# A transformer kernel's first stage: scale vectors spread by TensorE, transfers and splits reordered, first queries turned later

## What is computed

```python
def rms_norm(x, g):
    xf = x.astype(jnp.float32)
    y = xf * lax.rsqrt(jnp.mean(xf * xf, axis=-1, keepdims=True) + NORM_EPS)
    return (y * g.astype(jnp.float32)).astype(x.dtype)
...
mem_n = rmsnorm(mem, norm_mem[layer])
km, vm = jnp.split(mem_n @ w_kv, 2, axis=-1)
...
h = rms_norm(x, attn_norm_g[l])
proj = jnp.einsum('bsd,de->bse', h, w_in[l])
qa, ka, va, qb, kb, vb, f_logit, g_logit = jnp.split(proj, bounds, axis=-1)
qa = partial_rope(rms_norm(split_heads(qa, N_MOBA_HEADS), moba_q_norm_g[l]), pos)
```

## Time and profile before

| | us |
|---|---|
| median of 3 executions | 869.7 |
| lowest and highest | 868.4, 872.04 |
| the profiled execution | 871.05 |
| its span, first to last instruction | 868.8 |
| PE busy | 797.1 (92%) |
| DVE busy | 550.6 (63%) |
| ACT busy | 485.9 (56%) |
| POOL busy | 86.6 (10%) |

### The profile page before, as it was taken

How to read it: one execution, slowest core, us unless ns; L and a number is a source line. 1 busy time by engine, 2 the same in 40 slices (tenths; PEclk the granted TensorE clock), 3 DMA queues, 4 the chain that set the end, 5 groups by cost and what they waited for, 6 DMA issues and landing times.

```text
span 868.8 us, 10702 instructions
## 1 busy us (share of the span) xinstructions
PE 797.1 (92%) x3811; PEld 647.7 (75%) x3811; DVE 550.6 (63%) x817; ACT 485.9 (56%) x743; POOL 86.6 (10%) x50
## 2 busy tenths in 40 slices
PE   4989999999799999999999798796859999999998
PEld 3777788777588888888887577663637888888886
DVE  5676676567556777776463477687673666665650
ACT  4755656666236777774264744342543677776630
POOL 0023000000000000000000056644231000000000
PEclk9989999999999999999999899798969999999999
DMA  8766333344237655456383533221001675554550
GB/s 303 292 203 198 103 116 119 97 147 140 68 120 251 211 193 193 151 170 204 105 270 124 179 98 97 78 68 49 25 25 48 215 237 182 177 184 173 191 165 24
DMA packets 70566, 130.21 MB, mean 150 GB/s; under 512 B 5534, under 2 KB 17142, under 8 KB 70142
## 3 DMA queue, kind: packets, MB, share of 16 engines
q1 hardware_dynamic: 69662, 124.90, 44.2%
q10 hardware_dynamic: 864, 4.78, 1.5%
HBM read 128.61 MB, written 1.05 MB: 149 GB/s over the span
## 4 chain that ended last, share of the span: by engine, by line
PE 74%; DVE 11%; ACT 7%; DMA 4%; issue 2%; POOL 1%; SPq 1%; ACTq 0%; DVEq 0%; POOLq 0%
PE acc L478 20%; PE acc L480 20%; PE acc L479 20%; DMA b_raw<-in_w_in 2%; DVE b_wlo L1186 2%; PE banks L579 2%; PE banks L704 2%; PE banks L539 2%; PE banks L564 2%; PE banks L717 1%; DMA b_raw<-in_w_mem_kv 1%; ACT b_whi L825 1%; PE banks L552 1%; PE banks L543 1%; PE banks L566 1%
## 5 line engine op out<-in xcount | busy, mean ns | idle before, releaser
L1186 DVE TENSOR_TENSOR b_wlo<-b_raw,b_whi 128x1024 fp32r<-128x1024 f32 (+4 forms) x222 | 253.1, 1179 | 102.8 <-ACT b_whi L825 101.4
L825 ACT ACTIVATE b_whi<-b_raw 128x1024 fp32r<-128x1024 f32 (+4 forms) x244 | 234.3, 1001 | 77.1 <-DMA b_raw<-in_w_in 19.3
L478 PE MATMUL acc<-b_whi,b_hhi 128*128 128x512 f32 (+4 forms) x528 | 205.0, 388 | 10.3 <-DVE b_hlo L1459 4.6
L479 PE MATMUL acc<-b_whi,b_hlo 128*128 128x512 f32 (+4 forms) x528 | 198.2, 375 | 0.0
L480 PE MATMUL acc<-b_wlo,b_hhi 128*128 128x512 f32 (+4 forms) x528 | 197.8, 375 | 0.0
L478 PEld LDWEIGHTS acc<-b_whi,b_hhi 128*128 128x128 f32 x528 | 100.9, 191 | 31.0 <-DVE b_hlo L1459 5.1
L480 PEld LDWEIGHTS acc<-b_wlo,b_hhi 128*128 128x128 f32 x528 | 100.8, 191 | 15.8
L479 PEld LDWEIGHTS acc<-b_whi,b_hlo 128*128 128x128 f32 x528 | 100.8, 191 | 15.8 <-issue 1.5
L478 PE MATMUL acc<-b_whi,b_ohi 128*128 128x512 f32 (+1 forms) x272 | 105.8, 389 | 5.4 <-DVE b_wlo L1186 2.9
L480 PE MATMUL acc<-b_wlo,b_ohi 128*128 128x512 f32 (+1 forms) x272 | 103.4, 380 | 0.0
L479 PE MATMUL acc<-b_whi,b_olo 128*128 128x512 f32 (+1 forms) x272 | 103.1, 379 | 0.0
(11 more groups left out here) (214 smaller groups left out, 909.0 us busy)
## 6 DMA issues: line engine op xcount, KB each, us to landing
b_raw<-in_w_in SPq DMA_DIRECT2D x48, 512.0 KB, 4.8
b_raw<-in_w_ffn_up SPq DMA_DIRECT2D x40, 512.0 KB, 4.8
b_raw<-in_w_ffn_in SPq DMA_DIRECT2D x40, 512.0 KB, 4.7
b_raw<-in_w_ffn_down SPq DMA_DIRECT2D x22, 512.0 KB, 6.0
b_raw<-in_w_ffn_out SPq DMA_DIRECT2D x22, 512.0 KB, 4.7
b_raw<-in_w_out SPq DMA_DIRECT2D x16, 512.0 KB, 3.7
b_raw<-in_w_in SPq DMA_DIRECT2D x12, 412.0 KB, 3.6
b_raw<-in_w_in SPq DMA_DIRECT2D x8, 410.0 KB, 3.5
```

What stands on the lines that cost most here:

```text
L478: nc.tensor.matmul(o, a, wh, start=first, stop=False)
L479: nc.tensor.matmul(o, b, wh, start=False, stop=False)
L825: A(whi[:, n % SPLIT, 0:c["nk"], 0:c["n"]], raw[:, n % RAW, 0:c["nk"], 0:c["n"]], ACT.Copy)\
L1186: V.tensor_tensor(wlo[:, n % SPLIT, 0:c["nk"], 0:c["n"]], raw[:, n % RAW, 0:c["nk"], 0:c["n"]], whi[:, n % SPLIT, 0:c["nk"], 0:c["n"]].bit ...
```

## The change

The two scale vectors are loaded as one row of 4 KB each, issued by ACT. TensorE spreads each over 128 partitions, by a product of a row of ones (set by POOL) with it into the banks `acc[1]`, from which DVE reads it in `norm_gain`. TensorE also runs products of that row of ones whose results nobody reads (`idle`). The memory tokens are handled one token tile at a time on DVE and ACT, with a chunk's split behind each, and TensorE transposes the second tile between the products of the first. On SP, each memory tile goes before one of the first chunks, x behind chunk 3, the constants, `bf`, `og` and the head gains between chunks 6 and 7, the convolution's vectors before chunk 8, `pick` before chunk 20. The gate bias is issued by ACT ahead of moving va out. In `MIX1` the turning of qa stands behind the second half of va, and the convolution's vectors are transposed behind the turning of mk.

```diff
-        memg = gates[:, 0, D:2 * D]
+        memg = gates[0:1, 0, D:2 * D]
+        ones = rp.rearrange("p a t h d -> p (a t h d)")[0:1, :]
...
         MIX1 = [("gemm", "qa", 0), ("gemm", "qa", 1), ("sums", "qa"), ("gemm", "ka", 0), ("turn", "mk"),
-                ("gemm", "ka", 1), ("sums", "ka"), ("gemm", "va", 0), ("turn", "qa"), ("gemm", "va", 1), ("sums", "va"),
+                ("vectors", 0), ("gemm", "ka", 1), ("sums", "ka"), ("gemm", "va", 0), ("gemm", "va", 1), ("turn", "qa"),
+                ("sums", "va"),
                 ("gemm", "qb", 0), ("turn", "ka")]
...
+                        if between and t == 0:
+                            between()
+                            between = None
...
+            def spread(k, row):
+
+                pe.wait_ge(sem(f"{k} gain row in"), 16)
+                for b in range(2):
+                    mm = nc.tensor.matmul(acc[1][b][:, :], ones[:, 0:P], row[:, b * CN:(b + 1) * CN], start=True, stop=True)
+                mm.then_inc(sem(f"{k} gain spread"), 1)
+
+            def idle(n):
+
+                for _ in range(n):
+                    nc.tensor.matmul(acc[0][1][:, :], ones[:, 0:P], ones, start=True, stop=True)
+
+            def second_tile():
+
+                norm_T("mem", 0, [1])
+                norm_T("mem", 1, [1])
+
+            pe.wait_ge(sem("ones set"), 1)
+            idle(3)
+            spread("mem", memg)
+            idle(1)
             pe.wait_ge(sem("identity in"), 16)
-            norm_T("mem", 0)
-            norm_T("mem", 1)
-            gemm("mkv", 0, norm="mem")
+            norm_T("mem", 0, [0])
+            norm_T("mem", 1, [0])
+            idle(3)
+            gemm("mkv", 0, norm="mem", between=second_tile)
+            spread("x1", gain[0:1, :])
             norm_T("x1", 0)
             gemm("mkv", 1, norm="mem")
             norm_T("x1", 1)
-            pe.wait_ge(sem("vec in"), 32)
-            claim(0, "vecT")
-            full(nc.tensor.transpose(X[0][:, 0:4 * FT], vec[:, :], ident[0:4 * FT, 0:4 * FT]), 0, "vecT")
-            pe.wait_ge(sem("consts in"), 16)
...
+            memory = tokens(memx, "mem_2", "mem")
             for n, c in enumerate(chunks):
-                if n == PART:
-                    sp.dma_start(gain[:, :], dram["attn_norm_g"][0, :].partition_broadcast(P))\
-                      .then_inc(sem("gain in"), 16)
-                    for t in range(T):
-                        sp.dma_start(x[:, t, :], dram["x"][0, t * P:(t + 1) * P, :]).then_inc(sem(f"x {t} in"), 16)
+                if n < T:
+                    next(memory)
                 if n == RAW:
+                    for _ in tokens(x, "x", "x"):
+                        pass
+                if n == RAW + 3:
                     sp.dma_start(cst[:, P:], dram["consts"][:, P:]).then_inc(sem("consts in"), 16)
-                    sp.dma_start(vec[0:3 * FT, :], dram["ffn_conv_w"][0].rearrange("a (b p) -> (a b) p", p=P))\
-                       .then_inc(sem("vec in"), 16)
-                    sp.dma_start(vec[3 * FT:4 * FT, :], dram["ffn_conv_b"][0].rearrange("(b p) -> b p", p=P))\
-                       .then_inc(sem("vec in"), 16)
                     small(bf[:, :], "b_forget", "small in")
                     small(og[:, :], "hg_out_gain_2", "small in")
...
+                if n == groups["ka"]["first"]:
+                    sp.dma_start(vec[0:3 * FT, :], dram["ffn_conv_w"][0].rearrange("a (b p) -> (a b) p", p=P))\
+                       .then_inc(sem("vec in"), 16)
...
+                if n == groups["kb"]["first"]:
                     sp.dma_start(pick[:, :, :], dram["pick"]).then_inc(sem("pick in"), 16)
...
-            norm_hi("mem", ohi, 0)
-            norm_hi("mem", ohi, 1)
+            act.dma_start(memg, dram["norm_mem_2"]).then_inc(sem("mem gain row in"), 16)
+            act.dma_start(gain[0:1, :], dram["attn_norm_g"]).then_inc(sem("x1 gain row in"), 16)
+            for t in range(T):
+                norm_hi("mem", ohi, 0, [t])
+                norm_hi("mem", ohi, 1, [t])
+                hi_to(t)
             hi_to(2 * PART - 1)
...
-            for t in range(T):
-
-                act.wait_ge(*at("tokens scaled", "mem 1 1"))
-                act.dma_start(gates[:, t, :], dram["b_gate"][0].rearrange("a d -> (a d)").partition_broadcast(P))\
-                   .then_inc(sem("gate bias in"), 16)
...
+                    if n == "va":
+                        gate_bias()
...
+                done(V.tensor_tensor(xn[:, t, h], src[:, t, h], g[:, h] if k not in ("mem", "x1") else acc[1][b][:, :],
+                                     ALU.mult), "tokens scaled", f"{k} {t} {b}")
...
-            for b in range(2):
-                for t in range(T):
-                    norm_gain("mem", memx, memg, b, t, [(sem("memory gain in"), 16), (sem(f"mem {t} in"), 16)])
-            norm_lo("mem", ohi, olo, 0)
-            norm_lo("mem", ohi, olo, 1)
+            for t in range(T):
+                for b in range(2):
+                    norm_gain("mem", memx, None, b, t, [(sem("mem gain spread"), 1), (sem(f"mem {t} in"), 16)])
+                norm_lo("mem", ohi, olo, 0, [t])
+                norm_lo("mem", ohi, olo, 1, [t])
+                lo_to(t)
             lo_to(2 * PART - 1)
             for b in range(2):
                 for t in range(T):
-                    norm_gain("x1", x, gain, b, t, [gain_at(1), (sem(f"x {t} in"), 16),
+                    norm_gain("x1", x, None, b, t, [(sem("x1 gain spread"), 1), (sem(f"x {t} in"), 16),
                                                     at(f"bank{2 * t + b} full", "memT")])
...
+            G.memset(ones, 1.0).then_inc(sem("ones set"), 1)
```

More of the change, by code:

```diff
@@ L454, in full, with gemm @@
                 done(ins, f"bank{bank} full", step, i)
-            def gemm(name, c=None, i=0, norm=None):
+            def gemm(name, c=None, i=0, norm=None, between=None):
                 g = groups[name]
@@ L640, in _ @@
                           2 * len(T_BANKS[n]))
+                elif kind == "vectors":
+                    pe.wait_ge(sem("vec in"), 32)
+                    claim(0, "vecT")
+                    full(nc.tensor.transpose(X[0][:, 0:4 * FT], vec[:, :], ident[0:4 * FT, 0:4 * FT]), 0, "vecT")
+                    pe.wait_ge(sem("consts in"), 16)
                 elif kind == "decay sums":
@@ L769, in _, with tokens @@
         def _(sp):
-            sp.dma_start(ident, dram["consts"][:, C_ID:C_ID + P]).then_inc(sem("identity in"), 16)
-            sp.dma_start(memg, dram["norm_mem_2"][0, :].partition_broadcast(P)).then_inc(sem("memory gain in"), 16)
-            for t in range(T):
-                sp.dma_start(memx[:, t, :], dram["mem_2"][0, t * P:(t + 1) * P, :]).then_inc(sem(f"mem {t} in"), 16)
+            def tokens(dst, name, family):
+                for t in range(T):
+                    sp.dma_start(dst[:, t, :], dram[name][0, t * P:(t + 1) * P, :]).then_inc(sem(f"{family} {t} in"), 16)
+                    yield
             def small(dst, name, family):
                 sp.dma_start(dst, dram[name][0, :].partition_broadcast(P)).then_inc(sem(family), 16)
+            sp.dma_start(ident, dram["consts"][:, C_ID:C_ID + P]).then_inc(sem("identity in"), 16)
+            memory = tokens(memx, "mem_2", "mem")
             for n, c in enumerate(chunks):
-                if n == PART:
-                    sp.dma_start(gain[:, :], dram["attn_norm_g"][0, :].partition_broadcast(P))\
-                      .then_inc(sem("gain in"), 16)
-                    for t in range(T):
-                        sp.dma_start(x[:, t, :], dram["x"][0, t * P:(t + 1) * P, :]).then_inc(sem(f"x {t} in"), 16)
+                if n < T:
+                    next(memory)
                 if n == RAW:
+                    for _ in tokens(x, "x", "x"):
+                        pass
+                if n == RAW + 3:
                     sp.dma_start(cst[:, P:], dram["consts"][:, P:]).then_inc(sem("consts in"), 16)
-                    sp.dma_start(vec[0:3 * FT, :], dram["ffn_conv_w"][0].rearrange("a (b p) -> (a b) p", p=P))\
-                       .then_inc(sem("vec in"), 16)
-                    sp.dma_start(vec[3 * FT:4 * FT, :], dram["ffn_conv_b"][0].rearrange("(b p) -> b p", p=P))\
-                       .then_inc(sem("vec in"), 16)
                     small(bf[:, :], "b_forget", "small in")
@@ L845, in norm_squares, with norm_hi @@
                     done(A(junk, src[:, t, :], ACT.Square, accum_out=ss[:, rstd(k, t)]), "squares", f"{k} {t}")
-            def norm_hi(k, hi, b):
-                for t in range(T):
+            def norm_hi(k, hi, b, tiles=range(T)):
+                for t in tiles:
                     act.wait_ge(*at(f"bank{2 * t + b} full", f"{k}T"))
@@ L1025, in _, with gate_bias @@
             guess("mk", slice(0, T * 4))
-            act.wait_ge(*at("bank0 full", "vecT"))
-            done(A(vT[:, :], X[0][:, 0:4 * FT], ACT.Copy), "bank0 free", "vecT")
             root_in("x1")
```

(26 more changed lines are left out.)

3 lines of the change are left out of this document (2 added, 1 removed).

## The result

The changed kernel is **slower**, by 1.2%: 880.28 us median of six (877.69 to 883.8) against 869.05 of six for the kernel before; the ratio is 1.0116, with a 95% interval of 1.0093 to 1.0139. The forecast was 869.0, no change, within 865.0 to 873.0. The profiled execution of the changed kernel took 878.6 us.

The account below looks back on a forecast made before the run. PE, busy 92% of the span, was taken as the bound. First scores 1.8 us sooner, less 1.1 for the slow stretch, gave 0.7 won: 869.7 - 0.7 = 869.0 us, range 865.0 to 873.0.

Parts of the forecast that it names:

- the one on the first tokens: Kernel start: idle products raise PE's clock, the spread ends at 7.4, DVE starts then as before; nothing won, within 6.5 to 8.
- Rival 2: Kernel start: one-row products don't lift the clock, first product 4.2 later, 7 to 8 lost, 877 us; chance 0.1.
- The conv vectors' transfer, transpose (0.25) and copy (0.23) only move: Convolution's vectors, moved later: their work only changes place, two issues stand before chunk 8; nothing won or lost.
- of about 4 us at ka: Before the turning of ka: the stop at qa becomes one of about 4 us, waiting for ka's rope; 2.2 won there.
- The slow stretch behind the stop at ka: First scores and qb's second half at the low clock: 0.9 and up to 1.7, taken as 1.1 us.
- the net gain of 0.7 in the sum: At the first scores: 1.8 us won, 1.1 taken by the slow stretch, 0.7 left, nothing changed behind.
- The 13 us that the change could win at most: PE's stops before 80 us and their slow stretches: about 8.5 + 3 x 1.5 = 13 us, all the change can win.
- The gate bias: Beside the weights at 69 to 76: chunk 23 gets half the bandwidth, 1.3 us become 2.6; bounds nothing or 4 later.
- the split by tile with a warm clock: Memory tokens: first product of mkv at 12.2 against 15.29, first half through at 20.3 against 22.46, 2.2 won.
- the second spread gives it back: Before mkv's second half: spread 1.8 us on PE's path, then DVE's two scalings to 23.4; PE 0.6 later.
- SP's eleven issues: Between chunks 6 and 7 on SP: 5 to 9 us, taken as 6.5; chunk 7 lands at 29.5, 1.1 won.
- turning qa later alone wins nothing: Turning qa behind va's second half removes its 2.69 us stop, which becomes one of about 4 us at ka.

Follow-up runs that it names:

- run 1: The changed kernel without the seven idle products, the two spreads kept: 872.93 us, ratio 1.002 to the kernel before.
- run 4: The changed kernel with the idle products taken over 128 rows of ones instead of one: 872.05 us, ratio 1.0002 to the kernel before.
- run 2: The changed kernel with the convolution's vectors transposed into bank 3 instead of bank 0: 881.08 us, ratio 1.0127 to the kernel before.
- run 3: The changed kernel without idle products and with the convolution's vectors in bank 3: 872.37 us, ratio 1.0011 to the kernel before.
- run 7: The kernel before with qa turned behind va's second half and the gate bias issued ahead of moving va out: 871.64 us, ratio 1.001.
- run 8: The kernel before with qa turned later and the gate bias issued ahead of moving qb out: 868.74 us, ratio 0.9982.
- run 9: As run 3, with the gate bias issued ahead of moving qb out: 871.04 us, ratio 1.0009 to the kernel before.
- run 10: As run 9, but with the idle products kept, over 128 rows: 871.09 us, ratio 1.0009 to the kernel before.
- run 12: As run 11, with SP's small issues moved behind chunk 7: 864.53 us, ratio 0.9948 to the kernel before.
- run 11: As run 10, with x's scale vector spread by a transfer as in the kernel before: 867.76 us, ratio 0.9977 to the kernel before.
- run 5: The kernel before with only the turning of qa moved behind va's second half: 871.4 us, ratio 1.001.
- run 6: The kernel before with only the gate bias moved, issued ahead of moving va out: 870.56 us, ratio 0.999.

## Why the prediction was wrong

- **The step that failed first** is the one on the first tokens: "two idle products at 1.9, by when the clock should have risen". It never rose on one-row products. DVE started at 10.24, not 7.4, the first product came at 19.15, not 12.2. Rival 2 had this mechanism and its sizes right up to x's second half: first product at 19.5 (19.15), x's second half copied at 39 (39.67). Its 877 us stopped there, at 7 to 8 lost (8.1 measured); the first scores are 11.8 late and the time was 880.28. It got 0.1 of the chances and stood outside the range; its own remark that no row shows one-row products for long should have weighed more. Runs 1 and 4 show that this step is worth some 8 us.
- **A wait was overlooked.** "The conv vectors' transfer, transpose (0.25) and copy (0.23) only move": moved behind the turning of mk they claim the bank that mk's heads stand in, until ACT, behind qa's moving out and the splits of two more chunks, has copied them. 7.42 us. Taking it away won nothing (runs 2 and 3), as it covered the two stops for ka's rope and for chunk 22; but the working did not have it at all. It shows why nothing was seen of the stop "of about 4 us at ka": in the changed kernel ka's rope was ready at 85.3 and PE came at 89.36. In runs 2, 3, 7 to 10 and 12, without the stop at the vectors, that stop is there, with 2.69 to 3.93.
- **The slow stretch behind the stop at ka** was taken as 1.1 us of a possible 2.6. Where that stop stands, PE needed 1.8 to 3.3 us more from the first scores on than in the kernel before. With it the net gain of 0.7 in the sum is gone, even with a warm-up that works. (The 13 us that the change could win at most are summed with 1.5 per stop where the working has 1.7; nothing rests on it.)
- **The gate bias** was named at the right place and mis-sized: a chunk half as fast, 1.3 us, was the term, and 4.9 it was (6.12 in run 7 against 1.22 in run 8), beyond the bound of 4. The bias had the engines to itself first and then moved four times the chunk's bytes per packet. It concerned chunk 22 before chunk 23. In the changed kernel itself, with PE so late, ACT split both without waiting for them (86.17), so this term has no part in its loss; it has in runs 2 and 3.
- **Right, once the idle products work**: that nothing is won before DVE's first scaling (7.87 to 8.97 in runs 4 and 10 to 12, so 0.5 to 1.6 later than the 7.4 forecast, as the clock rose only behind all six passes, not after four; without any idle products it was 6.16 in run 1, which the sum did not see); the split by tile with a warm clock (first product 12.75 to 13.86 in these runs, 12.2 forecast, mkv's first half through at 21.1 to 22.3, 20.3 forecast); that the second spread gives it back (2.8 us in run 10; the sum had 1.8 + 1.3 of waiting); SP's eleven issues (6.5 forecast, 5.2 measured, from 28.19 to 33.41); that turning qa later alone wins nothing (run 5, 1.001), though the stop of 4 us at ka by which it was to be so was 1.38 in that trace. With the idle products mended, the kernel is where the forecast put it (872.05, ratio 1.0002). That is luck in part: its first scores stand at 83.56, not 77.6, behind a stop of 7.87 that the sum did not have.
- **SP's issues**: ACT waited only 0.18 for chunk 7 in the changed kernel, so SP's issues played no part in its loss; they did as soon as PE was early (run 11).

## What to carry to other kernels

Work that is meant to warm TensorE should look like the real work, rows included: here the same products with one row left the clock low for 18 us and made everything behind it late. Whoever moves a transpose or product to another place in PE's order asks who frees its bank there, and when in that engine's own order. A bulk load on a second queue can more than double the time to landing of a load that an in-order engine is about to wait for (8.4 us instead of 3.7 here): put it where no one waits. And a stop that is moved is paid twice, as time and as the low clock behind it: judge a change some way behind the stop, not at it.

## What the runs showed of the hardware that was not expected

- 18 passes of 512 columns with one row, from 1.30 to 19.15 us, at 0.86 to 0.92 us each, with eight transposes between them, and the clock stayed low; with 128 rows it rose in the first six passes or just behind them (six took 4.61 to 5.49 in runs 4 and 10 to 12, and the four of the spread behind them 1.98 to 2.21). The column of the granted clock read 1.00 all the same: at the start of these traces the durations are what tells the level.
- While both had packets to move, two queues shared the DMA engines by packets, 76 to 63, and thus by bytes 0.61 to 0.13 MB; before that, a chunk issued 0.9 us behind the first of two 1 MB transfers moved 2 packets in 4 us, against their 184.
- The kernel before differed by up to 12.6 us between executions on one chip (865.0 to 877.64). The start of one trace is no sure measure either: the kernel before and runs 5 to 8 run the same program up to the first product, and it stands at 15.29, 14.75, 16.08, 14.56 and 15.00.
